# Four half-tile weight slots, with the low part in place of the raw weights, in the stages of a single-core mixer kernel that still load whole tiles

## The reference, cut to what matters

```python
for l in range(DEPTH):
    h = modulate(rms_norm(x, norm1_g[l]), mod[0], mod[1])
    hc = modulate(rms_norm(xc, norm1_g[l]), modc[0], modc[1])
    y, yc = token_mixer(h, hc, w_in[l], conv_w[l], ..., w_dn_out[l], w_out[l], not last)
    x = x + mod[2][:, None, :] * y
    h = modulate(rms_norm(x, norm2_g[l]), mod[3], mod[4])
    x = x + mod[5][:, None, :] * peer(h, peer_w_q[l], peer_key1[l], peer_key2[l], peer_u[l], peer_v[l])
```

## Time and profile before

| | |
|---|---|
| three runs | 4217.30, 4221.48 and 4224.32 us, median 4221.48 |
| the profiled execution | 4223.51 us |
| its span | 4221.4 us (2.1 us lie around it) |
| PE busy | 4111.1 us, 97% of the span |
| DVE, ACT busy | 2976.7 us (71%), 1977.9 us (47%) |
| DMA | 200 GB/s over the span, 60.4% of 16 engines |

### The profile page before, as it was taken

How to read it: one execution, slowest core, us unless ns; L and a number is a source line. 1 busy time by engine, 2 the same in 40 slices (tenths; PEclk the granted TensorE clock), 3 DMA queues, 4 the chain that set the end, 5 groups by cost and what they waited for, 6 DMA issues and landing times. The chain is left out here.

```text
span 4221.4 us, 66175 instructions
## 1 busy us (share of the span) xinstructions
PE 4111.1 (97%) x24351; PEld 3591.3 (85%) x24351; DVE 2976.7 (71%) x5007; ACT 1977.9 (47%) x2942; POOL 318.8 (8%) x654
## 2 busy tenths in 40 slices
PE   7999999999989999999999999999999999999999
PEld 1888889779988999888888888888888888988899
DVE  5887886876866677578866666666666578876746
ACT  1542224537643344444455554444444465454644
POOL 0000000000566600000000000000000100300000
PEclk9999999999999999999999999999999899999999
DMA  9673433468863357556665556777777455554564
GB/s 381 233 284 131 149 140 125 159 232 297 268 207 119 106 221 260 188 183 212 212 191 183 181 183 214 237 242 242 242 239 247 159 173 170 157 166 155 175 196 159
DMA packets 271300, 846.30 MB, mean 200 GB/s; under 512 B 74192, under 2 KB 112352, under 8 KB 234736
## 3 DMA queue, kind: packets, MB, share of 16 engines
q1 hardware_dynamic: 271088, 843.40, 60.4%
HBM read 792.85 MB, written 50.45 MB: 200 GB/s over the span
## 5 line engine op out<-in xcount | busy, mean ns | idle before, releaser
L251 DVE TENSOR_TENSOR rounded<-arena,rounded 128x1024 fp32r<-128x1024 f32 x792 | 975.3, 1232 | 498.6 <-ACT rounded L245 496.1
L245 ACT ACTIVATE rounded<-arena 128x1024 fp32r<-128x1024 f32 x792 | 839.5, 1061 | 769.3 <-DMA arena<-in_peer_v 358.5
L2547 PE MATMUL bank<-rounded,rounded 128*128 128x512 f32 x2048 | 524.5, 398 | 0.5 <-ACT rounded L245 0.5
L3396 PE MATMUL bank<-rounded,rounded 128*128 128x512 f32 x1856 | 473.7, 397 | 4.6 <-DVE rounded L3841 2.9
L2547 PEld LDWEIGHTS bank<-rounded,rounded 128*128 128x128 f32 x2048 | 367.0, 189 | 66.5 <-issue 0.6
L2937 PE MATMUL bank<-rounded,rounded 128*128 128x512 f32 x1024 | 398.9, 390 | 2.8 <-PEq L155 2.8
L2938 PE MATMUL bank<-rounded,rounded 128*128 128x512 f32 x1024 | 398.8, 389 | 0.0
L3396 PEld LDWEIGHTS bank<-rounded,rounded 128*128 128x128 f32 x1856 | 334.9, 190 | 66.4 <-issue 4.7
L2552 PEld LDWEIGHTS bank<-rounded,rounded 128*128 128x128 f32 x2048 | 279.0, 189 | 21.4
L2552 PE MATMUL bank<-rounded,rounded 128*128 128x256 f32 x2048 | 285.1, 282 | 0.0
L2941 PE MATMUL bank<-rounded,rounded 128*128 128x512 f32 x1024 | 274.5, 390 | 0.0
(11 more groups left out here) (506 smaller groups left out, 7858.1 us busy)
## 6 DMA issues: line engine op xcount, KB each, us to landing
arena<-in_w_in SPq DMA_DIRECT2D x128, 1024.0 KB, 5.0
arena<-in_peer_u SPq DMA_DIRECT2D x256, 512.0 KB, 3.9
arena<-in_peer_v SPq DMA_DIRECT2D x256, 512.0 KB, 4.5
arena<-in_w_in SPq DMA_DIRECT2D x232, 512.0 KB, 3.6
arena<-in_w_mod SPq DMA_DIRECT2D x80, 1024.0 KB, 8.0
arena<-in_w_out SPq DMA_DIRECT2D x48, 512.0 KB, 3.6
arena<-in_w_conv_out SPq DMA_DIRECT2D x16, 1024.0 KB, 4.9
arena<-in_w_dn_out SPq DMA_DIRECT2D x16, 1024.0 KB, 5.2
```

The costliest lines, as they stand in the source:

```text
L245: act.activation(k.half(0, r, q), k.raw_half(r, q), ACT.Copy).then_inc(k.hi_done, 1)
L251: dve.tensor_tensor(k.half(1, r, q), k.raw_half(r, q), k.half(0, r, q), ALU.subtract).then_inc(k.lo_done, 1)
L2547: pe.matmul(k.ps[r][:], part(0, m), flat(k.r(pair_slot + 2 * kt, 2)), start=(kt == 0), stop=False, skip_group_check=True)
L3396: pe.matmul(both, part(0, m), hi_lo(kt), start=(kt == 0), stop=False, skip_group_check=True)
```

## The change

In the five stages with split weights the ring of two raw tiles and the two staging halves give way to the four half slots that the later stages use. The high part of half (j, q) goes to its own slots 16 + 8 (j % 2) + 4 q, the low part over the raw half in slots 8 (j % 2) + 4 q. A load is 512 KB instead of 1 MB, waits for `half_done` of half i-4 instead of `lo_done` of tile j-2, and has a semaphore for each of four slots. `high(i)` waits for half i-4 instead of half i-2. The loops of ACT, DVE and PE keep their order. `load_next` does the same for the two tiles ahead of the next stage; the two conv tiles that `query_stage` loads as raw tiles wait for `half_done` too. In `delta_prepare` each half load stands behind the side DMAs of its own half.

```diff
 def half_high(k, act, g, r, q, s):
-    act.wait_ge(k.half_loaded[2 * (r % 2) + q], g * 32 + (16 * ((s + r - k.halves_from) // 2) + 16))
+    act.wait_ge(k.half_loaded[2 * (r % 2) + q], g * 32 + (16 * ((s + r) // 2) + 16))
     act.activation(k.half(0, r, q), k.raw_half(r, q), ACT.Copy).then_inc(k.hi_done, 1)
...
+def load_half(k, sp, w, r, q, need):
+    if need is not None:
+        sp.wait_ge(k.half_done, need + q)
+    sp.dma_start(k.raw_half(r, q), w[:, q * 1024:(q + 1) * 1024]).then_inc(k.half_loaded[2 * (r % 2) + q], 16)
 def load_halves(k, sp, w, r, need):
     for q in range(2):
-        if need is not None:
-            sp.wait_ge(k.half_done, need + q)
-        sp.dma_start(k.raw_half(r, q), w[:, q * 1024:(q + 1) * 1024]).then_inc(k.half_loaded[2 * (r % 2) + q], 16)
+        load_half(k, sp, w, r, q, need)
 def load_next(k, sp, following, s_end):
     for r in range(2):
-        sp.wait_ge(k.lo_done, 2 * (s_end - 2 + r) + 2)
-        sp.dma_start(k.raw(r), following[r]).then_inc(k.raw_loaded[r], 16)
+        load_halves(k, sp, following[r], r, 2 * (s_end - 2 + r) + 1)
...
             for j in range(2, tiles):
-                sp.wait_ge(k.lo_done, 2 * (s + j - 2) + 2)
-                sp.dma_start(k.raw(j % 2), w[j]).then_inc(k.raw_loaded[j % 2], 16)
+                load_halves(k, sp, w[j], j, 2 * (s + j - 2) + 1)
...
-                part = lambda p, m: k.staged(p, q)[:, m * P:(m + 1) * P]
+                part = lambda p, m: k.half(p, j, q)[:, m * P:(m + 1) * P]
...
             def high(j, q):
-                if q == 0:
-                    act.wait_ge(k.raw_loaded[j % 2], 16 * ((s + j) // 2) + 16)
-                act.wait_ge(k.half_done, 2 * (s + j) + q - 1)
-                act.activation(k.staged(0, q), k.raw(j % 2)[:, q * 1024:(q + 1) * 1024], ACT.Copy).then_inc(k.hi_done, 1)
+                if s + j >= 2:
+                    act.wait_ge(k.half_done, 2 * (s + j - 2) + q + 1)
+                half_high(k, act, 0, j, q, s)
...
             def low(j, q):
                 dve.wait_ge(k.hi_done, 2 * (s + j) + q + 1)
-                dve.tensor_tensor(k.staged(1, q), k.raw(j % 2)[:, q * 1024:(q + 1) * 1024], k.staged(0, q),
-                                  ALU.subtract).then_inc(k.lo_done, 1)
+                dve.tensor_tensor(k.half(1, j, q), k.raw_half(j, q), k.half(0, j, q), ALU.subtract).then_inc(k.lo_done, 1)
...
             for r in range(2):
-                sp.wait_ge(k.lo_done, 2 * (s + tiles - 2 + r) + 2)
+                sp.wait_ge(k.half_done, 2 * (s + tiles - 2 + r) + 2)
                 sp.dma_start(k.raw(r), w_next[r]).then_inc(k.plain_loaded[r], 16)
...
             for j in range(tiles):
-                for i in (2 * j - 5, 2 * j - 4):
+                for q, i in enumerate((2 * j - 4, 2 * j - 3)):
                     for h in at_half(i, 2):
...
-                if j >= 2:
-                    sp.wait_ge(k.lo_done, 2 * (s + j - 2) + 2)
-                    sp.dma_start(k.raw(j % 2), w[j]).then_inc(k.raw_loaded[j % 2], 16)
+                    if j >= 2:
+                        load_half(k, sp, w[j], j, q, 2 * (s + j - 2) + 1)
```

More of the change, by code:

```diff
@@ L1007, in load @@
                 else:
-                    sp.dma_start(k.raw(j % 2), following3[j - tiles]).then_inc(k.raw_loaded[j % 2], 16)
+                    load_halves(k, sp, following3[j - tiles], j, None)
             def scales(p):
@@ L2068, in weight_high @@
             def weight_high(q):
-                act.wait_ge(k.raw_loaded[k.raws % 2], 16 * (k.raws // 2) + 16)
-                act.activation(k.staged(0, q), k.raw(0)[:, q * 1024:(q + 1) * 1024], ACT.Copy).then_inc(k.hi_done, 1)
+                half_high(k, act, 0, 0, q, k.raws)
             for h in range(HEADS):
@@ L2204, in _ @@
                     dve.wait_ge(k.hi_done, 2 * k.raws + 1)
-                    dve.tensor_tensor(k.staged(1, 0), k.raw(0)[:, 0:1024], k.staged(0, 0), ALU.subtract).then_inc(k.lo_done, 1)
+                    dve.tensor_tensor(k.half(1, 0, 0), k.raw_half(0, 0), k.half(0, 0, 0), ALU.subtract).then_inc(k.lo_done, 1)
                     inverse(h - 1)
@@ L2267, in _ @@
                     sp.dma_start(k.iota, k.i["cst"][:, 256 + 16 * P:256 + 17 * P]).then_inc(k.keys_in, 16)
-            k.halves_from = s + tiles
-            for r in range(2):
-                sp.wait_ge(k.lo_done, 2 * (s + tiles - 2 + r) + 2)
-                load_halves(k, sp, following3[r], r, None)
+            load_next(k, sp, following3, s + tiles)
             sp.wait_ge(k.saved, 64)
```

24 lines of the change are left out of this document (8 added, 16 removed).

## The result

The changed kernel takes **4247.8 us** (median of four runs, 4244.6 to 4254.0), the kernel before 4222.1 in the runs beside it: a ratio of 1.0065, 95% interval 1.0052 to 1.0077. It is 0.65% slower. The forecast was 4208.6, range 4201 to 4219; both the sign and the range were wrong. All ratios and intervals here are of fast executions; the single slow one, of experiment 6, took 14,466 us at a granted clock of 0.29.

What follows compares the result with a forecast made beforehand. It took PE, 97% busy, as the bound, with waits from late loads and from ACT and DVE not allowed far enough ahead. Terms summed to 12.9 us off the 4221.5 us median, giving 4208.6 us, range 4201 to 4219.

Steps and rivals of the forecast that it cites:

- (I): First and kv stage, copies, subtractions and added DMA issues: nothing gained or lost, as those stages have no waits to lose.
- (G): Output stage: DVE's row-sum steps and one wait at half 33 get a half more room, gain 2.2 us.
- (A): Delta preparation: PE's waits for a load or its copy mostly go, gain 5.5 us, bounds 2 and 8.
- (E): Last step of the inverse: inverse_out(3) queues behind 512 KB instead of 1 MB, gain 0.3 us, bounds -2 and 2.
- (C): Delta preparation, ACT at the gates, halves 66 to 80: a start further ahead stops ACT pacing PE, gain 0.8 us.
- (D): Delta preparation, inverse from half 79: DVE enters with a lead of some 3.3 us instead of 0.8, gain 2.7 us.
- first rival: Delta preparation: DMA engines stay the bound in the crowded stretch, DVE at the inverse; gain 3.2 us, 4218 us, chance 20%.
- (B): Delta preparation, about 1090 to 1125 us: three waits for DVE behind a head's work go, gain 1.9 us.
- (F): End of delta preparation: SP waits for the last product, then issues its last loads, reaching the barrier later, loss 1.0 us.
- unit: A half of 24 matmuls takes 2.88 us; each wait costs 0.25 to 0.3 us beyond its idle time.
- rule against the change: The skill's advice of 1 MiB or more per DMA; the forecast gave small transfers no extra price.
- The third: Rival: in delta preparation's crowded stretch the smaller loads land too late, slower, 4229 us, chance 4%.

Runs made afterwards that it cites:

- experiment 6: Kernel before, whole tiles and old slots, with the kv rows, x, block and inverse_out loads moved in SP's order: 4215.3 us, ratio 0.9993.
- Experiment 1: Changed kernel with the row loads issued ahead of the weight half loads in first, kv and output stage: 4230.3 us, ratio 1.0019.
- experiment 7: Kernel of experiment 5 with w_ab ahead of the first stage's last half load, and taps, later inverse_out and blocks spread: 4208.4 us, ratio 0.9977.
- experiment 3: Kernel before with each row load of first, kv and output stage held until half 2j-2 was multiplied: 4258.8 us, ratio 1.0094.
- experiment 5: Kernel of Experiment 1 with kv rows, x, block and inverse_out loads moved apart in SP's order: 4210.7 us, ratio 0.9983.
- experiment 8: Kernel of experiment 7 with ACT's eight gates reordered and ended earlier: 4203.3 us, ratio 0.9958; repeated unchanged, 4204.2 us, ratio 0.9957.
- experiment 4: Kernel before with each 1 MB weight load of the five stages issued as two DMAs of 512 KB: 4227.6 us, ratio 1.0018.

## Why the prediction was wrong

**The step that failed is (I)**, "first and kv stage have no waits to lose, and their loads 7.3 us or more to land". It put both stages at nothing; they measured -11.5 and -2.6 us. It looked at the weight loads alone and asked if they still land in time. They did. It did not ask what is queued *behind* the load on SP: the row pieces, 1 MB each, which inherit its wait, and at the kv stage's start `w_ab`. The same step failed in **(G)**, which put the output stage at +2.2 and measured -10.7. The first and the output stage together are -22 us against +2.2; as far as the output stage's length can be told, see above. Experiment 1 (order turned: 20 us of the two stages' 22 back) shows the cause there, and experiment 7 (`w_ab` ahead: its wait from 2.40 to 0.26 us) that at the kv stage's start; experiment 3 (old slots, rows late: the same waits) supports it from the other side, with late weights beside the rows. The remark that PE starting to wait in the first stage would make the forecast wrong was right, but had no price, since DVE's five waits for `in_w_mod` in the trace of before, 8.6 us in all, had not been read as a queue that already stood at its edge.

**(A)**, load waits of delta preparation, +5.5 put: the waits in the quiet stretches did go, with that for half 4 (1.45 us), which was to stay, but those of the crowded one grew from 4.1 us (three, 1054 to 1072) to 6.6. "7% of 27 us is all that can be made up there" took a DMA share of 0.93 for a bound. It is not one: experiment 5 ran 50 us at 0.98 with PE waiting 0.3, and 27 us of it (1041.4 to 1068.4) read 1.05 at 308 GB/s, so 1 isn't even the top of that column. What counted was that two block loads and up to two head transfers stood in a row between pairs of half loads. Taken apart, the stage gained 12.4 us, more than A's upper bound of 8, but that has two terms in it: 6.7 us of idle time before high parts are gone (about 8 with refill, an estimate at 0.3 us a wait), and the last wait of 2.75 us, which is E's.

**(C) and (D)**, +3.5 together: nothing. The price of a lead was misjudged twice. It does not build, since ACT at the gates does not get ahead of PE, and DVE enters with 0.74 us instead of the 3.3 put (0.73 in the old slots of experiment 6, so the slots give none of it; experiment 8 gets 3.39 when the gates are moved); and where it is there, it delays the first of the five waits and saves 0.2 us of their idle time, as DVE's rate decides the rest. The first rival said as much of D.

**(B)**, +1.9: nothing; the waits behind the heads' work are 0.60 and 0.45 us, at 1118.9 and 1132.6, where they were 0.66 and 0.45 (two in the trace, not the three put). **(E)**, +0.3: the last wait is 3.23 us against 2.75, so -0.5. **(F)**, -1.0, was right: the gap before the scan's first instruction is 2.33 us against 1.31. **(H)**, +0.5: nothing; the query stage has the same waits, 1.5 us. The **unit** held in the first stage: six waits, 9.6 us more of idle time, cost 11.5 us, 0.3 each beyond the idle time (0.25 to 0.3 put). In the output stage 5.7 us of added idle time went with 10.7, so there it did not, with the scatter named above. In the rule against the change, the two landings of the trace do not stand nearer together in ratio than the two estimates beside them: 5.0 to 3.6 is 1.39, 4.4 to 3.2 is 1.38. Nothing hung on it, but the price of nothing for small transfers was too low (experiment 4).

**The rivals.** The third, slower, had the right sign and the wrong loads: it let the weights be late in the crowded stretch (12.1 us landing). The half loads there landed in 8.8 us at most, and PE's idle time there grew by 2.5 us; the loss was elsewhere. At 4% it was held too unlikely, and "slower" had no other mechanism at all, though the change puts a later wait in front of everything that SP issues in five stages.

## What to carry to other kernels

When a wait is changed on a queue that issues in order, list what stands behind it up to the next wait, and give each of those transfers a deadline of its own: here a 1 MB side load that landed 3 us later cost more than the weights' new slots could bring. A trace of before that already shows short waits for such a transfer says that there is no room left. And a smaller slot needs smaller neighbours: with loads of 512 KB, taking side loads apart that stood two to four in a row was the difference between 4230 and 4211 us, 14.8 us of it in delta preparation.

## What the runs showed of the hardware

A DMA share of 0.93 in a stretch was not the engines' limit: the stretch with the blocks ran at 0.98 and 303 GB/s when the issues were spread, and the column can read above 1 (1.05). SP stood 3.0 to 5.0 us at the issue behind two transfers in 128-byte runs, in the kernel before as in the changed one, and at most 2.2 us behind one of them (experiment 5), so a half load whose wait is long over still goes out late. Two DMAs of 512 KB in place of one of 1 MB landed after 4.8 and 5.1 us against 4.8 to 5.0 in a quiet stretch, and cost, over the 176 tiles, 6.5 us of time. And a wait of 2.3 us is sometimes followed by a lower clock: after the wait of 2.29 us at 312 us in experiment 1 the granted clock of the stretch is 0.91 and the kv stage 4.2 us longer, while after 2.31 us at 322.5 us in the changed kernel it is 1.00 and the stage 2.6 us longer. The stretches 300 to 320 us of experiment 1 and 320 to 340 us of the changed kernel:

```profile
300.00:320.00 20.00, 17.71 (x83) 14.63 (x82) 11.78 (x25) 8.04 (x12) 0.00 (x0) 0.91 0.69 241
```

```profile
320.00:340.00 20.00, 17.69 (x79) 14.32 (x78) 15.70 (x34) 6.51 (x7) 0.00 (x0) 1.00 0.59 216
```

The idle time is the same and the price is not; what decides it these runs don't show.
